# Two more gather slots in the latents' residual buffer for the first 56 gathers, and the residual loaded at step 30

## The chip, the cores and the metric

One Trainium2 chip, one of its cores. The metric is the device time of one execution in microseconds, median of the runs shown; lower is better. The engines are TensorE (PE in the profile), VectorE (DVE), ScalarE (ACT), GpSimd (POOL) and SyncE (SP, which here only issues transfers). The data is float32 throughout.

## The reference, cut to what matters

One inference layer over two sequences: 128 context tokens (the prompt) and 512 latent tokens (the sample), 640 tokens in all, in five blocks of 128. Each token goes through a token mixer (an SSM and a short gated convolution) and then through PEER, a retrieval of single-neuron experts:

```python
def layer(x, cond, h0_f, h0_b, rows, p):
    sh1, sc1, g1, sh2, sc2, g2 = [m.astype(x.dtype) for m in modulation(cond, p["w_mod"], p["b_mod"])]
    h = rmsnorm(x, p["norm1_g"]) * (1 + sc1) + sh1
    y, h_f, h_b = token_mixer(h, h0_f, h0_b, rows, p)
    x = x + g1 * y                                   # the residual that the change is about
    h = rmsnorm(x, p["norm2_g"]) * (1 + sc2) + sh2
    x = x + g2 * peer(h, p["w_query"], p["sub_keys"], p["expert_u"], p["expert_v"])
    return x, h_f, h_b

def block(xb):                                       # peer, one block of 128 tokens
    q = (xb @ w_query)...                            # 8 heads, two halves
    s = jnp.einsum("thse,sne->thsn", q, sk)
    ...                                              # top 16 of each half, then top 16 of the 256 sums
    gate = jax.nn.softmax(top, axis=-1)
    hid = jnp.einsum("thkd,td->thk", expert_u[idx], xb).astype(jnp.float32)
    act = (jax.nn.gelu(hid) * gate).astype(xb.dtype)
    return jnp.einsum("thk,thkd->td", act, expert_v[idx])
```

For every block, head and rank k one row of 2048 numbers (expert_u and expert_v of one expert, 8 KB) is fetched for each of 128 tokens. That is 5 x 8 x 16 = 640 gathers of 1 MB.

## The kernel before, in words

The program is written by hand, engine by engine; each engine runs its list in order and waits on semaphores. There are three stages.

The first (to about 213 us) computes the modulation, the SSM's matrices, the context's mixer and the context's residual. The second is the PEER of the context block (G = 0 to 7, one G for each head) with the latents' mixer laid between its pieces. The third is the PEER of the four latent blocks (G = 8 to 39).

**The gathers.** GpSimd issues the 640 gathers in order (L1890), each into one of SLOTS = 8 slots of 8 KB per partition in `r1`: gather j goes into slot j modulo 8. Before it is issued, GpSimd waits until `v_done` says that the slot's last row is used up. VectorE takes the first half of each row in a dot product with the token's hidden vector (`dot`, L1707), which waits for the row to land. Two rows make a pair. ScalarE applies GELU (L1258), VectorE weighs the pair (`weigh`, L1716 and L1719), and TensorE adds the second halves into two banks (`add_rows`, L846), which sets `v_done`. So a row's slot is free when TensorE has done its pair. In this text pair n holds gathers 2n and 2n + 1; a head has 8 pairs.

**The latents' mixer between them.** In the context block TensorE does, after the matmuls of pair n, step n of `latent_front`: a slice of the latents' projections (L930, L951), and from step 28 a slice of the output projection (L964). It also computes the next heads' queries there: `query(u)` (L781) needs the weights of head u, which are loaded into one buffer, `wqb`. VectorE has its own `latent_front(n)` after its dots; at n = 36 it forms for the first time residual + gate x output (L1788), in the buffer `xtl`, after a wait for `ld_xl`.

**SyncE's list.** All other loads are issued by SyncE in one fixed order with waits between them. The latents' residual `xtl` (2 MB, 128 x 8 runs of 512 numbers) is loaded when the context's output projection no longer needs its place (`zoc_mm` of 2): `xtl` shares the upper 4096 columns of `x_r` with half of the output weights, `woB`. Then follow the query weights of heads 1 and 2 (L443) and, for n = 0 to 63, the loads of `w_tiles` (L449), of query weights at n = 5, 13, 21, 29 (head n // 8 + 3) and of `w_o` (L453, n = 34 to 37). The query weights are 1 MB as 128 x 8 runs of 256 numbers. Each of these waits until its buffer is free; heads 2 to 8 wait for the previous query (`q_mm`).

Of the kernel before, what the change touches and what calls it, by code (L numbers as in the profile page):

```python
# [8 lines left out]
ALU = mybir.AluOpType  # L9
# [70 lines left out]
def build(nc, xT, condT, cols, w_mod, w_u, w_tiles, w_o, ssm, bc, dskip, skT, w_query, table, y_out, st_out, kfull):  # L80
    ctx = ExitStack()
    with ctx:
# [14 lines left out]
        def part(r, a, n):  # L97
            return r[:, a:a + n]
# [57 lines left out]

        rows = part(r1, 0, SLOTS * 2 * D).rearrange("p (s x) -> p s x", s=SLOTS)
        peer = part(r2, 0, 1024)
# [71 lines left out]
        ld_dsk = sem("ld_dsk")  # L230
        ld_sk = sem("ld_sk")
        ld_woa = sem("ld_woa")
        ld_wob = sem("ld_wob")
        ld_wob0 = sem("ld_wob0")
        ld_xc = sem("ld_xc")
        ld_xl = sem("ld_xl")
        ld_wq0 = sem("ld_wq0")
        ld_wq = sem("ld_wq")
# [115 lines left out]
        wtl_in = [sem(f"wtl_in{i}") for i in range(3)]  # L354
        row_in = [sem(f"row_in{i}") for i in range(SLOTS)]

# [17 lines left out]
        def _(sp):  # L374
# [24 lines left out]
            sp.dma_start(dsk[0:NCH, :], dskip).then_inc(ld_dsk, 16)  # L399
            sp.dma_start(sk[:, :, :], skT).then_inc(ld_sk, 16)  # L400
            for n in range(8, 18):
# [16 lines left out]
            sp.wait_ge(m_mm, 2)  # L418
            sp.dma_start(wqa, w_query[:, :, 0:DQ]).then_inc(ld_wq0, 16)
            for q in range(8, 10):  # L420
                load_conv_ctx(q)
            sp.wait_ge(mod_mm, 24)
            sp.dma_start(woA, w_o[:, 0:4, :, :]).then_inc(ld_woa, 16)
            for q in range(10, 12):
                load_conv_ctx(q)
            sp.wait_ge(zc_mm, 10)
            sp.dma_start(woB[:, 2:4, :, :], w_o[:, 6:8, :, :]).then_inc(ld_wob0, 16)
            sp.wait_ge(zc_mm, 12)
            sp.dma_start(woB[:, 0:2, :, :], w_o[:, 4:6, :, :]).then_inc(ld_wob, 16)
            sp.wait_ge(scan_ctx, 1)  # L430
            sp.dma_start(st_out, fin[:, :, :]).then_inc(st_dma, 16)
            sp.wait_ge(zoc_mm, 2)
            sp.dma_start(xtl, xT[:, :, CTX:T]).then_inc(ld_xl, 16)

# [47 lines left out]
        def _(pe):  # L482
# [276 lines left out]

            pe.wait_ge(ld_woa, 16)  # L760
            pe.wait_ge(ld_wob0, 16)
            out_ctx(True, range(KS), 1)
# [22 lines left out]
            def first_query():  # L785

                pe.wait_ge(ld_wq0, 16)
                for k in range(KD):
                    if k < KS:
                        pe.wait_ge(h_ready, KD + k + 1)  # L790
                    elif k == KS:
                        pe.wait_ge(xsc_ready, 2)
                    for h in range(2):
                        last = mm(bank[2][:, h * P:(h + 1) * P], wqa[:, k, h * P:(h + 1) * P], hT[:, k, 0:CTX], start=(k == 0 and h == 0),
                                  stop=(k == KD - 1), skip_group_check=True)
                last.then_inc(q_mm, 1)
# [39 lines left out]
            def add_rows(G, g):  # L836

                b = G // HEADS
                if G % HEADS == 0 and g == 0:
                    pe.wait_ge(h2c_ready, NH2 * (b + 1))  # L840
                pe.wait_ge(wgt_ready, NPR * G + g + 1)
                for h in range(2):
                    for e in range(2):
                        k = 2 * g + e
                        to = TG * ((k + 2 * h) % NTG)
                        last = mm(bank[ACC[b % 2][h]][to:to + TG, :], wgt[:, g % 2, e, :], rows[:, k % SLOTS, D + h * 512:D + (h + 1) * 512],  # L846
                                  start=(G % HEADS == 0 and k < NTG), stop=(G % HEADS == HEADS - 1 and k >= TOPK - NTG))
                        if h:
                            last.then_inc(v_done, 1)
# [177 lines left out]

            pe.wait_ge(ld_sk, 16)
            first_query()
# [51 lines left out]
        def _(act):  # L1081
# [200 lines left out]
            def take_sums(b):  # L1282

                act.wait_ge(v_done, (b + 1) * HEADS * TOPK + SLOTS)
# [116 lines left out]
        def _(dve):  # L1401
# [299 lines left out]
            def dot(G, par, k):  # L1701

                s, tg = k % SLOTS, k % NTG
                if G % HEADS == 0 and k < NTG:
                    dve.wait_ge(h2c_ready, G // HEADS * NH2 + tg + 2)
                dve.wait_ge(row_in[s], G * 32 + (k // SLOTS + 1) * 16)
                V.tensor_tensor_reduce(rows[:, s, 0:D], rows[:, s, 0:D], h2r[tg], 1.0, 0.0, ALU.mult, ALU.add,  # L1707
                                       hid[:, par, k:k + 1]).then_inc(dot_done, 1)

            def weigh(G, par, g):  # L1710

                n = NPR * G + g
                wl = Chain(dve, act_done, n)
                dve.wait_ge(gelu_done, n + 1)
                a = gel[:, par, 2 * g:2 * g + 2]
                wl(tt(a, a, gate[:, par, 2 * g:2 * g + 2], ALU.mult))  # L1716
                if n >= 2:
                    dve.wait_ge(v_done, 2 * (n - 1) + SLOTS)
                tt(wgt[:, g % 2, :, :], fold[:, :].rearrange("p (a m) -> p a m", a=1).broadcast_to([P, 2, TG]),  # L1719
                   a.rearrange("p (g m) -> p g m", m=1).broadcast_to([P, 2, TG]), ALU.mult).then_inc(wgt_ready, 1)  # L1720
# [111 lines left out]
            fl(V.tensor_copy(eyes[:, 1, 64:P], ident[:, 0:64]))  # L1832
            dve.wait_ge(v_done, NALL * TOPK + SLOTS)
            for h in range(2):
# [20 lines left out]
        def _(pool):  # L1855
# [12 lines left out]
            for a in range(2):  # L1868
                for b in range(2):
# [12 lines left out]
                           ident[:, :].rearrange("p (g s i) -> p g s i", g=NTG, s=1).broadcast_to([P, NTG, 4, TG])).then_inc(consts, 1)  # L1882
            pool.sem_inc(v_done, SLOTS)
            for G in range(NALL):
                e = G % 2
                pool.wait_ge(topk_done, G + 1)
                for k in range(TOPK):
                    pool.wait_ge(v_done, G * TOPK + (k + 1))
                    pool.nop(nofuse=True)
                    G_.indirect_dma_start(rows[:, k % SLOTS, :], None, table,  # L1890
                                          bass.IndirectOffsetOnAxis(gidx[:, e, k:k + 1], 0)).then_inc(row_in[k % SLOTS], 16)
    return nc
# [62 lines left out]
```

## Time and profile before

| | |
|---|---|
| median of 3 runs | 1960.12 us |
| lowest and highest | 1955.56 and 1962.29 us |
| span of the profiled execution | 1954.5 us |
| own time of the profiled execution | not given beside its span |
| PE, DVE, ACT, POOL busy | 61%, 73%, 19%, 37% |
| gathered | 671.13 of 745.91 MB |

The span runs from the first to the last instruction. The times are of whole executions, so the median is 5.6 us above this span; what lies between them holds the start and the end of the program and the difference between one execution and another. Part 2 of the page shows the span in 40 slices of 48.9 us; in it the transfer engines stand at 9 (90% or more) from slice 6 to the last but one. A share of 1.00 in a row of windows means that the 16 transfer engines were busy throughout.

### The profile page before, as it was taken

To read this page: it belongs to the slowest core of one execution; us is meant where nothing else is said; L and a number is where in the kernel's file an instruction comes from. 1 tells how busy PE (TensorE), PEld (TensorE's weight loads), DVE (VectorE), ACT (ScalarE), POOL (GpSimd) and SP (SyncE) were. 2 spreads that over 40 slices of the span, in tenths; PEclk is the share of its full clock that TensorE was granted. 3 is DMA by queue.
4 is the path that set the end of the run, shared out by engine and by line. 5 is a ranking of instruction groups with operands and counts; after the bars stand their busy time and mean duration, and the time that the engine had idled before them with its cause. 6 is when DMAs were issued, how large, how long until landed. Compare 5 with 4: busy or idle time off the path is not lost.

```text
span 1954.5 us, 22601 instructions
## 1 busy us (share of the span) xinstructions
PE 1197.1 (61%) x7716; PEld 476.1 (24%) x7716; DVE 1423.2 (73%) x3894; ACT 373.2 (19%) x845; POOL 717.9 (37%) x666
## 2 busy tenths in 40 slices
PE   6999888999767767774553434453444454444434
PEld 3569544444322322220110000111000011111001
DVE  8978557777766776667777777777777678877775
ACT  5242431221122111111211011121111111211010
POOL 0000233333333333334444444444444444344442
PEclk9999999999878777775755555565555565555555
DMA  8556799999999999999999999999999999999996
GB/s 347 179 196 220 275 358 401 373 396 415 401 368 374 404 414 401 397 401 393 421 421 422 419 410 416 412 412 412 416 413 415 417 412 415 415 410 419 412 409 254
DMA packets 126243, 745.91 MB, mean 382 GB/s; under 512 B 12128, under 2 KB 34912, under 8 KB 40624
## 3 DMA queue, kind: packets, MB, share of 16 engines
q0 software_dynamic: 92160, 671.13, 83.8%
q1 hardware_dynamic: 33968, 73.35, 10.5%
q8 instruction: 60, 0.98, 0.2%
q14 instruction: 55, 0.45, 0.1%
HBM read 741.78 MB, written 2.65 MB: 381 GB/s over the span
## 4 chain that ended last, share of the span: by engine, by line
DMA 33%; PE 30%; DVE 24%; issue 10%; ACT 1%; SPq 0%; DVEq 0%; POOL 0%; POOLq 0%; ACTq 0%
DMA r<-table,gidx 29%; DVE r L1707 8%; PE bank L846 7%; PE bank L814 6%; PE bank L951 3%; DMA r<-w_query 3%; PE bank L964 2%; PE bank L543 2%; DMA r<-w_u 2%; PE bank L781 1%; DVE wgt L1719 1%; DVE i L1649 1%; DVE r L1675 1%; DVE i L1655 1%; DVE r L1650 1%
## 5 line engine op out<-in xcount | busy, mean ns | idle before, releaser
L1890 POOL DMA_INDIRECT r<-table,gidx x640 | 709.7, 1109 | 1053.1 <-PE bank L846 891.0
L1707 DVE CUSTOM_DVE_ANT_0 r<-r 128x1024 f32<-128x1024 f32 x640 | 780.3, 1225 | 310.4 <-DMA r<-table,gidx 292.8
L846 PE MATMUL bank<-r,wgt 128*32 128x512 f32 x2560 | 532.2, 916 | 711.3 <-DVE wgt L1719 692.2
L846 PEld LDWEIGHTS bank<-r,wgt 128*32 128x32 f32 x2560 | 61.3, 130 | 1078.5 <-DVE wgt L1719 1011.3
L1258 ACT ACTIVATE r<-r 128x2 f32<-128x2 f32 x320 | 65.1, 204 | 1033.3 <-DVE r L1707 1016.4
L814 PE MATMUL bank<-hT_r,r 128*128 128x512 f32 x256 | 120.1, 624 | 0.9 <-ACT hT_r L1112 0.9
L1716 DVE TENSOR_TENSOR r<-r 128x2 f32<-128x2 f32 x320 | 50.1, 157 | 68.5 <-ACT r L1258 68.5
L1719 DVE TENSOR_TENSOR wgt<-fold,r 128x64 f32<-128x64 f32 x320 | 72.0, 225 | 11.1
L814 PEld LDWEIGHTS bank<-hT_r,r 128*128 128x128 f32 x256 | 50.0, 200 | 75.1 <-issue 75.1
L1258 ACT ACT_TABLE_LOAD x51 | 65.4, 1283 | 0.9
L964 PE MATMUL bank<-mix_r,r 128*128 128x512 f32 x128 | 61.0, 619 | 0.0
L951 PE MATMUL bank<-hT_r,r 128*128 128x512 f32 x128 | 60.8, 619 | 0.0
L832 PEld LDWEIGHTS bank<-r,ident 128*32 128x32 f32 x1280 | 43.0, 139 | 46.6 <-DVE r L1686 39.8
L1707 DVE DVE_READ_ACCUMULATOR2_ANT r<- 128x1 f32 x640 | 52.8, 83 | 0.0
L1254 ACT ACT_TABLE_LOAD x40 | 51.3, 1283 | 0.7
L871 PE MATMUL bank<-mix_r,modrow 128*128 128x512 f32 x80 | 47.4, 730 | 3.2 <-ACT r L1273 1.9
L832 PE MATMUL bank<-r,ident 128*32 128x8 f32 x1280 | 46.7, 195 | 1.5 <-DVE r L1686 1.5
L1648 DVE MAX8 r<-r 128x8 f32<-128x128 f32 x80 | 19.3, 284 | 23.8 <-ACT r L1250 15.9
L1875 POOL MEMSET r<- 128x2048 f32 x1 | 1.8, 1812 | 92.8 <-DVE sv L1506 92.8
L1254 ACT ACTIVATE r<-r,small 128x16 f32<-128x16 f32 x40 | 12.3, 308 | 114.8 <-DVE pos L1668 114.8
L543 PE MATMUL bank<-hT_r,r 128*128 128x512 f32 x64 | 32.5, 654 | 2.2 <-DMA r<-w_u 2.2
L781 PE MATMUL bank<-hT_r,r 128*128 128x128 f32 x224 | 29.3, 288 | 6.5 <-DMA r<-w_query 6.5
(356 smaller groups left out, 1438.5 us busy)
## 6 DMA issues: line engine op xcount, KB each, us to landing
r<-w_mod SPq DMA_DIRECT2D x24, 1024.0 KB, 8.2
r<-w_query SPq DMA_DIRECT2D x15, 1024.0 KB
r<-table,gidx POOLq DMA_INDIRECT x640, 11.7
r<-w_tiles SPq DMA_DIRECT2D x12, 512.0 KB, 8.2
x_r<-w_tiles SPq DMA_DIRECT2D x10, 512.0 KB, 5.9
hT_r<-xT SPq DMA_DIRECT2D x4, 640.0 KB, 5.9
r<-w_u SPq DMA_DIRECT2D x1, 2048.0 KB, 29.9
r<-w_o SPq DMA_DIRECT2D x1, 2048.0 KB, 10.9
```

Source lines behind the costliest of these rows:

```text
L543: last = mm(bank[m][:, :], wu[:, k, m * P:(m + 1) * P], hT[:, k, CTX:T], start=(k == 0), stop=(k == KD - 1))
L814: last = mm(bank[2 + h][:, :], wqb[:, k, h * P:(h + 1) * P], hT[:, k, CTX:T], start=(k == 0), stop=(k == KD - 1))
L832: last = mm(bank[3][TG * s:TG * s + TG, 8 * tg:8 * tg + 8], ident[:, TG * tg:TG * tg + TG], gi[:, :, 4 * s:4 * s + 4], start=True, stop=True)
L846: last = mm(bank[ACC[b % 2][h]][to:to + TG, :], wgt[:, g % 2, e, :], rows[:, k % SLOTS, D + h * 512:D + (h + 1) * 512], start=(G % HEADS = ...
L951: last = mm(bank[(4, 5, 7)[r]][:, :], wtl[(tile + 2) % 3][:, k, :], hT[:, k, CTX:T], start=(k == 0), stop=(k == KD - 1))
L964: last = mm(bank[OUT_BANK[m % 3]][:, :], woA[:, m % 4, k, :], mixl[:, k, :], start=(k == 0), stop=(k == KD - 1))
L1254: A(e16, top, ACT.Exp, bias=small[:, 0:1], accum_out=small[:, 1:2]).then_inc(exp_done, 1)
L1258: A(gel[:, par, 2 * g:2 * g + 2], hid[:, par, 2 * g:2 * g + 2], ACT.Gelu_apprx_tanh).then_inc(gelu_done, 1)
L1707: V.tensor_tensor_reduce(rows[:, s, 0:D], rows[:, s, 0:D], h2r[tg], 1.0, 0.0, ALU.mult, ALU.add, hid[:, par, k:k + 1]).then_inc(dot_done, 1)
L1716: wl(tt(a, a, gate[:, par, 2 * g:2 * g + 2], ALU.mult))
L1719: tt(wgt[:, g % 2, :, :], fold[:, :].rearrange("p (a m) -> p a m", a=1).broadcast_to([P, 2, TG]), a.rearrange("p (g m) -> p g m", m=1).bro ...
L1890: G_.indirect_dma_start(rows[:, k % SLOTS, :], None, table, bass.IndirectOffsetOnAxis(gidx[:, e, k:k + 1], 0)).then_inc(row_in[k % SLOTS], 16)
```

## The change

Two more slots are made out of the place of `xtl`. A table that is made when the program is built (`slot_ring`) gives each gather its slot, the slot's use count and the gather that had it before. Gathers 0 to 55 go round 10 slots, the rest round 8. For the first 56 gathers the slot of gather j was last held by gather j - 10. Gathers 56 and 57 take over slots from 46 and 47, gather 58 from 50, and from there the previous holder is always j - 8, as before. The last gather in one of the two extra slots is 49.

The load of `xtl` goes from its place after `zoc_mm` to SyncE's step n = 30, behind the query weights of n = 29, with a wait for `v_done` of 50. The first gather into each extra slot waits for `zoc_mm` of 2 instead. Some semaphores are merged (`ld_sk` with `ld_wq0`, `ld_woa` with `ld_wob0`) and the starting credit of 8 on `v_done` goes away, with every wait on it lowered by 8.

```diff
+EARLY = 2
+EARLY_TO = 56
+def slot_ring(total):
+    last, slot, use, prev = {}, [], [], []
+    for j in range(total):
+        s = min(range(SLOTS + EARLY if j < EARLY_TO else SLOTS), key=lambda i: last.get(i, i - SLOTS - EARLY))
+        slot.append(s)
+        use.append(slot.count(s))
+        prev.append(last.get(s))
+        last[s] = j
+    return slot, use, prev
...
-        rows = part(r1, 0, SLOTS * 2 * D).rearrange("p (s x) -> p s x", s=SLOTS)
+        rows = [part(r1, 2 * D * i, 2 * D) for i in range(SLOTS)] + [part(x_r, D, 2 * D), part(x_r, 3 * D, 2 * D)]
+        SLOT, USE, PREV = slot_ring(NBLK * HEADS * TOPK)
...
-            sp.wait_ge(zoc_mm, 2)
-            sp.dma_start(xtl, xT[:, :, CTX:T]).then_inc(ld_xl, 16)
...
+                if n == 30:
+                    sp.wait_ge(v_done, max(j for j in range(EARLY_TO) if SLOT[j] >= SLOTS) + 1)
+                    sp.dma_start(xtl, xT[:, :, CTX:T]).then_inc(ld_xl, 16)
...
-            pe.wait_ge(ld_woa, 16)
-            pe.wait_ge(ld_wob0, 16)
+            pe.wait_ge(ld_wo, 32)
...
-                dve.wait_ge(row_in[s], G * 32 + (k // SLOTS + 1) * 16)
-                V.tensor_tensor_reduce(rows[:, s, 0:D], rows[:, s, 0:D], h2r[tg], 1.0, 0.0, ALU.mult, ALU.add,
+                dve.wait_ge(row_in[SLOT[j]], USE[j] * 16)
+                V.tensor_tensor_reduce(row, row, h2r[tg], 1.0, 0.0, ALU.mult, ALU.add,
...
-            pool.sem_inc(v_done, SLOTS)
...
-                    pool.wait_ge(v_done, G * TOPK + (k + 1))
+                    j = G * TOPK + k
+                    if PREV[j] is not None:
+                        pool.wait_ge(v_done, PREV[j] + 1)
+                    elif SLOT[j] >= SLOTS:
+                        pool.wait_ge(zoc_mm, 2)
```

SyncE's list before, from the loads of the context's output weights to the last `w_tiles`. The residual is `x_r<-xT 128x8x512`, the query weights are `w_query`:

```order
L429 DMA x_r<-w_o 128x2048 [waits zc_mm]
L431 DMA st_out<-fin 128x64 [waits scan_ctx]
L433 DMA x_r<-xT 128x8x512 [waits zoc_mm]
L443 DMA r<-w_query 128x8x256 [waits yl_mm]
L443 DMA r<-w_query 128x8x256 [waits q_mm]
L449 DMA mix_r<-w_tiles 128x1024
```

And the same list after the change, with the end of this stretch:

```order
L442 DMA x_r<-w_o 128x2048 [waits zc_mm]
L444 DMA st_out<-fin 128x64 [waits scan_ctx]
L454 DMA r<-w_query 128x8x256 [waits yl_mm]
...
L460 DMA r<-w_tiles 128x1024 [waits zl_mm] x2
L454 DMA r<-w_query 128x8x256 [waits q_mm] x2
L475 DMA x_r<-xT 128x8x512 [waits v_done]
L464 DMA r<-w_o 128x1024 [waits zol_mm] x4
L454 DMA r<-w_query 128x8x256 [waits q_mm] x2
```

The residual has moved past two loads of query weights in front of it, twelve of `w_tiles` and four more of query weights, to just behind the query weights of n = 29 and ahead of the four pieces of `w_o`.

GpSimd's list before, from the first gather:

```order
L1890 DMA r<-table,gidx 128x2048 [waits topk_done,v_done]
L1890 DMA r<-table,gidx 128x2048 [waits v_done] x15
L1890 DMA r<-table,gidx 128x2048 [waits topk_done,v_done]
L1890 DMA r<-table,gidx 128x2048 [waits v_done] x15
```

And after; a gather into `x_r` is one into an extra slot:

```order
L1906 DMA r<-table,gidx 128x2048 [waits topk_done]
L1906 DMA r<-table,gidx 128x2048 x7
L1906 DMA x_r<-table,gidx 128x2048 [waits zoc_mm] x2
L1906 DMA r<-table,gidx 128x2048 [waits v_done] x6
L1906 DMA r<-table,gidx 128x2048 [waits topk_done,v_done]
L1906 DMA r<-table,gidx 128x2048 [waits v_done]
L1906 DMA x_r<-table,gidx 128x2048 [waits v_done] x2
```

Gathers 8 and 9 no longer wait for the first pair's matmuls but only for `zoc_mm`; the order of the gathers is the same.

## Rows read from the trace of the kernel before

**Rows 1.** The page, parts 2 and 4: slices of the span, and the last chain.

```profile
DMA  8556799999999999999999999999999999999996
GB/s 347 179 196 220 275 358 401 373 396 415 401 368 374 404 414 401 397 401 393 421 421 422 419 410 416 412 412 412 416 413 415 417 412 415 415 410 419 412 409 254
DMA 33%; PE 30%; DVE 24%; issue 10%; ACT 1%; SPq 0%; DVEq 0%; POOL 0%; POOLq 0%; ACTq 0%
```

**Rows 2.** Windows: stretch, busy us of each engine, clock, transfer share, GB/s.

```profile
200.00:213.00 13.00, 12.18 (x280) 10.21 (x281) 8.67 (x37) 5.91 (x10) 0.00 (x0) 1.00 0.02 4
255.00:280.00 25.00, 23.98 (x143) 12.97 (x143) 11.26 (x33) 5.39 (x11) 8.66 (x8) 0.97 0.83 305
280.00:320.00 40.00, 38.17 (x205) 18.20 (x205) 31.14 (x79) 8.68 (x17) 13.89 (x13) 1.00 1.02 415
320.00:380.00 60.00, 53.58 (x254) 23.93 (x251) 40.76 (x107) 10.96 (x22) 19.31 (x18) 0.94 0.97 368
416.00:424.00 8.00, 8.00 (x31) 2.87 (x24) 3.55 (x8) 0.77 (x3) 4.22 (x4) 1.00 0.99 351
424.00:450.00 26.00, 23.92 (x137) 9.97 (x136) 23.59 (x73) 7.29 (x14) 12.15 (x11) 1.00 1.01 421
450.00:505.00 55.00, 53.49 (x274) 27.10 (x273) 37.62 (x98) 9.09 (x22) 19.07 (x18) 0.97 1.02 415
700.00:1925.00 1225.00, 587.59 (x3229) 149.42 (x3227) 903.61 (x2526) 176.06 (x429) 530.57 (x477) 0.57 1.01 412
```

**Rows 3.** The last chain in order of time: start, us, what; pieces of it.

```profile
225.68 26.98 DMA r<-w_query
252.70 3.78 PE bank L781 x16
...
377.23 30.00 DMA r<-w_query
407.27 2.05 PE bank L781 x16
...
715.25 9.72 DMA r<-table,gidx
```

**Rows 4.** Waits of DVE, 225 to 452 us: us, times, longest.

```profile
DVE r L1707 <- DMA r<-table,gidx: 1.6, 2, 1.3
```

**Rows 5.** Waits of DVE, 700 to 1925 us.

```profile
DVE r L1707 <- DMA r<-table,gidx: 248.0, 233, 2.2
```

**Rows 6.** Waits of PE, 225 to 452 us.

```profile
PE bank L781 <- DMA r<-w_query: 6.5, 2, 5.0
```

**Rows 7.** Timeline of SP: start, us, what (x2: first to last issue).

```profile
190.23 0.55 SPq L433 DMA_DIRECT2D x_r<-xT  x1
...
377.23 39.08 SPq L443 DMA_DIRECT2D r<-w_query  x2
```

**Rows 8.** Transfer queues, 226 to 252 us: packets, MB, share.

```profile
q0 software_dynamic: 1193, 8.66, 80.3%
q1 hardware_dynamic: 1309, 2.03, 21.6%
```

**Rows 9.** Transfer queues, 416 to 424 us.

```profile
q1 hardware_dynamic: 1031, 1.04, 41.7%
```

**Rows 10.** Timeline of PE around 407 us; in brackets idle before, and releaser.

```profile
402.09 3.70 PE L951 MATMUL bank<-hT_r,r 128*128 128x512 f32 x8
407.27 2.05 PE L781 MATMUL bank<-hT_r,r 128*128 128x128 f32 x16 [1.48 <-DMA r<-w_query]
```

**Rows 11.** Timeline of DVE, 448 to 465 us.

```profile
448.92 1.40 DVE L1788 SCALAR_TENSOR_TENSOR x_r<-bank,modT,x_r 128x512 f32<-128x512 f32 x2
...
452.15 1.22 DVE L1707 CUSTOM_DVE_ANT_0 r<-r 128x1024 f32<-128x1024 f32 x1 [0.70 <-DMA r<-table,gidx]
...
457.60 1.23 DVE L1707 CUSTOM_DVE_ANT_0 r<-r 128x1024 f32<-128x1024 f32 x1 [3.21 <-DMA r<-table,gidx]
...
461.20 1.23 DVE L1707 CUSTOM_DVE_ANT_0 r<-r 128x1024 f32<-128x1024 f32 x1 [2.37 <-DMA r<-table,gidx]
...
462.54 0.22 DVE L1719 TENSOR_TENSOR wgt<-fold,r 128x64 f32<-128x64 f32 x1
```

**Rows 12.** Timeline of PE, 459 to 464 us.

```profile
459.15 3.70 PE L964 MATMUL bank<-mix_r,r 128*128 128x512 f32 x8
462.82 1.06 PE L846 MATMUL bank<-r,wgt 128*32 128x512 f32 x8
```

**Rows 13.** Timeline of POOL, the eighth, ninth and fifteenth gather.

```profile
222.57 0.94 POOL L1890 DMA_INDIRECT r<-table,gidx  x1 [0.30 <-issue]
232.85 1.20 POOL L1890 DMA_INDIRECT r<-table,gidx  x1 [9.34 <-PE bank L846]
...
258.34 0.94 POOL L1890 DMA_INDIRECT r<-table,gidx  x1 [10.34 <-PE bank L846]
```

**Rows 14.** The page, part 6: median us from issue to landing.

```profile
r<-table,gidx POOLq DMA_INDIRECT x640, 11.7
```

More of the change, by code:

```diff
@@ L230, in build @@
         ld_dsk = sem("ld_dsk")
-        ld_sk = sem("ld_sk")
-        ld_woa = sem("ld_woa")
+        ld_wo = sem("ld_wo")
         ld_wob = sem("ld_wob")
-        ld_wob0 = sem("ld_wob0")
         ld_xc = sem("ld_xc")
         ld_xl = sem("ld_xl")
-        ld_wq0 = sem("ld_wq0")
+        ld_first = sem("ld_first")
         ld_wq = sem("ld_wq")
@@ L354, in build @@
         wtl_in = [sem(f"wtl_in{i}") for i in range(3)]
-        row_in = [sem(f"row_in{i}") for i in range(SLOTS)]
+        row_in = [sem(f"row_in{i}") for i in range(SLOTS + EARLY)]
         NPR = TOPK // 2
@@ L399, in _ @@
             sp.dma_start(dsk[0:NCH, :], dskip).then_inc(ld_dsk, 16)
-            sp.dma_start(sk[:, :, :], skT).then_inc(ld_sk, 16)
+            sp.dma_start(sk[:, :, :], skT).then_inc(ld_first, 16)
             for n in range(8, 18):
@@ L418, in _ @@
             sp.wait_ge(m_mm, 2)
-            sp.dma_start(wqa, w_query[:, :, 0:DQ]).then_inc(ld_wq0, 16)
+            sp.dma_start(wqa, w_query[:, :, 0:DQ]).then_inc(ld_first, 16)
             for q in range(8, 10):
@@ L422, in _ @@
             sp.wait_ge(mod_mm, 24)
-            sp.dma_start(woA, w_o[:, 0:4, :, :]).then_inc(ld_woa, 16)
+            sp.dma_start(woA, w_o[:, 0:4, :, :]).then_inc(ld_wo, 16)
             for q in range(10, 12):
@@ L426, in _ @@
             sp.wait_ge(zc_mm, 10)
-            sp.dma_start(woB[:, 2:4, :, :], w_o[:, 6:8, :, :]).then_inc(ld_wob0, 16)
+            sp.dma_start(woB[:, 2:4, :, :], w_o[:, 6:8, :, :]).then_inc(ld_wo, 16)
             sp.wait_ge(zc_mm, 12)
@@ L785, in first_query @@
             def first_query():
-                pe.wait_ge(ld_wq0, 16)
+                pe.wait_ge(ld_first, 32)
                 for k in range(KD):
@@ L845, in add_rows @@
                         to = TG * ((k + 2 * h) % NTG)
-                        last = mm(bank[ACC[b % 2][h]][to:to + TG, :], wgt[:, g % 2, e, :], rows[:, k % SLOTS, D + h * 512:D + (h + 1) * 512],
+                        last = mm(bank[ACC[b % 2][h]][to:to + TG, :], wgt[:, g % 2, e, :], rows[SLOT[G * TOPK + k]][:, D + h * 512:D + (h + 1) * 512],
                                   start=(G % HEADS == 0 and k < NTG), stop=(G % HEADS == HEADS - 1 and k >= TOPK - NTG))
@@ L1026, in turn_last @@
                         last.then_inc(pt_mm, 1)
-            pe.wait_ge(ld_sk, 16)
             first_query()
@@ L1282, in take_sums @@
             def take_sums(b):
-                act.wait_ge(v_done, (b + 1) * HEADS * TOPK + SLOTS)
+                act.wait_ge(v_done, (b + 1) * HEADS * TOPK)
                 if b:
@@ L1701, in dot @@
             def dot(G, par, k):
-                s, tg = k % SLOTS, k % NTG
+                j, tg = G * TOPK + k, k % NTG
+                row = rows[SLOT[j]][:, 0:D]
                 if G % HEADS == 0 and k < NTG:
                     dve.wait_ge(h2c_ready, G // HEADS * NH2 + tg + 2)
-                dve.wait_ge(row_in[s], G * 32 + (k // SLOTS + 1) * 16)
-                V.tensor_tensor_reduce(rows[:, s, 0:D], rows[:, s, 0:D], h2r[tg], 1.0, 0.0, ALU.mult, ALU.add,
+                dve.wait_ge(row_in[SLOT[j]], USE[j] * 16)
+                V.tensor_tensor_reduce(row, row, h2r[tg], 1.0, 0.0, ALU.mult, ALU.add,
                                        hid[:, par, k:k + 1]).then_inc(dot_done, 1)
@@ L1717, in weigh @@
                 if n >= 2:
-                    dve.wait_ge(v_done, 2 * (n - 1) + SLOTS)
+                    dve.wait_ge(v_done, 2 * (n - 1))
                 tt(wgt[:, g % 2, :, :], fold[:, :].rearrange("p (a m) -> p a m", a=1).broadcast_to([P, 2, TG]),
@@ L1832, in _ @@
             fl(V.tensor_copy(eyes[:, 1, 64:P], ident[:, 0:64]))
-            dve.wait_ge(v_done, NALL * TOPK + SLOTS)
+            dve.wait_ge(v_done, NALL * TOPK)
             for h in range(2):
@@ L1887, in _ @@
                 for k in range(TOPK):
-                    pool.wait_ge(v_done, G * TOPK + (k + 1))
+                    j = G * TOPK + k
[3 more added lines that the diff above has]
+                        pool.wait_ge(zoc_mm, 2)
                     pool.nop(nofuse=True)
-                    G_.indirect_dma_start(rows[:, k % SLOTS, :], None, table,
-                                          bass.IndirectOffsetOnAxis(gidx[:, e, k:k + 1], 0)).then_inc(row_in[k % SLOTS], 16)
+                    G_.indirect_dma_start(rows[SLOT[j]], None, table,
+                                          bass.IndirectOffsetOnAxis(gidx[:, e, k:k + 1], 0)).then_inc(row_in[SLOT[j]], 16)
     return nc
```

## The prediction

> **What bounds the kernel now.** I read the page first. The transfer engines are at 90% or more from the sixth slice on and move 400 to 420 GB/s in most slices after the fifteenth [rows 1], so a change that moves transfers looks as if it touched the bound. But the last chain gives DMA only 33% of the span, PE 30% and DVE 24% [rows 1], so the bound must change on the way. I therefore took the chain in order of time. From 213 to about 700 us its pieces are almost all PE and DVE; the only transfers in it are two loads of query weights, at 225.68 and 377.23 us [rows 3]. The first gathered row in it stands at 715.25 us [rows 3], and from there on rows alternate with short compute to the end. The waits say the same. Between 225 and 452 us VectorE, which takes the rows, waited for one only twice, 1.6 us in all [rows 4]. Between 700 and 1925 us it waited 233 times, 248.0 us [rows 5].
>
> So there are two regimes. In the last 1225 us the transfers bind: share 1.01, 412 GB/s [rows 2]. In the context's heads (213 to some 550 us) TensorE's list binds: it is busy 38.17 of 40 us and 53.49 of 55 us in two of the windows [rows 2], with the latents' mixer laid between the pairs. The transfer engines are nearly full there too, but have holes: 305 GB/s in 255 to 280, 368 in 320 to 380, 351 in 416 to 424 [rows 2]. The change acts in that second regime only. What it does to the end is what it does to the moment at which the compute chain hands over to the transfers, near 700 us.
>
> **The change part by part.**
>
> *Two more slots.* Before, GpSimd issued the eighth gather at 222.57 us and then waited 9.34 us for the first pair's matmuls; the fifteenth waited 10.34 us and was issued at 258.34 [rows 13]. Now gathers 8 and 9 follow at once and every pair until 28 is issued one pair earlier. That fills holes: at 415 GB/s as in the full window 280 to 320 [rows 2], those of 255 to 280 and 320 to 380 are worth 25 x (1 - 305/415) = 6.6 us and 60 x (1 - 368/415) = 6.8 us. But the lead can never be more than the two rows, 2.1 MB or 5.05 us, and nobody waits for it: VectorE's waits for rows here sum to 1.6 us [rows 4], and neither stands on the chain. Bounds 0 and -1.6 us; I take 0. The lead also ends by itself. Gather 58 waits for the matmuls of gather 50, as it did before, so the lead is spent by about 395 us.
>
> *The query weights behind the gathers.* TensorE waits twice for them, 6.5 us in all, 5.0 us of it before 252.70 [rows 3, 6]. Does a longer queue of gathers make this worse? In 226 to 252 us the gathers' queue had 1193 packets and SyncE's 1309, though 8.66 MB against 2.03 MB [rows 8]: while both have work they take turns piece by piece, 8 KB against 1 KB. A load of 1024 pieces waits its 1024 turns however many gathers stand behind, so two more don't lengthen it, and the 5.0 us stay. Bounds: 0 to +5 us (two rows, if the load had to wait for both); I take 0, by the counts. The second wait is 1.48 us before 407.27 [rows 10]. Its load was on its way from 377.23 for 30.00 us [rows 3]. Now the gathers' queue runs dry under it for a few us, since rows up to 57 were moved early and gather 58 is held as before; without gathers in between, the load gets through faster. Bounds 0 and -1.5 us; I take -1.5.
>
> *The residual's load.* Before it was issued at 190.23 us [rows 7] into idle engines (200 to 213 us: share 0.02, [rows 2]) and cost nothing. Now it is issued behind the second of the two query loads of the row at 377.23, that is at 377.23 + 39.08 = 416.3 us [rows 7]. Its wait for `v_done` of 50 is over by then, since pair 24 is long done, so nothing behind it on SyncE's queue (the `w_o` pieces) waits longer to be issued. It is 2.10 MB, at 421 GB/s of the window behind [rows 2] 5.0 us of transfer time in a stretch that was full: 421 and 415 GB/s until 505 us [rows 2]. What was idle there after 416 us: 8 x (1 - 351/421) = 1.3 us. So 5.0 - 1.3 = 3.7 us of it push rows back. Who waits for those rows? From 452 us on VectorE does: 0.70, 3.21 and 2.37 us [rows 11]. And there TensorE has no slack: the pair that VectorE weighed at 462.54 was taken at 462.82, the moment the matmuls before it ended [rows 11, 12]. So I count the 3.7 us in full. Bounds: 0 (the slack of VectorE over TensorE takes it up) and +5.0 us.
>
> *The residual itself.* VectorE needs it at 448.92 us [rows 11]. The query weights in front of it were through at 424: 1.04 of their 1.05 MB moved in 416 to 424 [rows 9], in the hole. From there 1024 pieces take turns with the gathers, as did the 1 MB load that took 26.98 us [rows 3]; 2 KB pieces instead of 1 KB add 1.05 MB or 2.5 us. 27.0 + 2.5 = 29.5 us from issue, of which about 2 us lie before the first byte, so it lands near 424 + 27.5 = 451.5 us, some 3 us late (4 if the chain came there 1.5 us early). VectorE then stands, with its dots behind, but these had waited 0.70 + 3.21 us for their rows anyway [rows 11]. Bounds 0 and +15 us (rival C); I take +0.5.
>
> The rule that bears on this is in the Trainium skill, DMA: Bandwidth & Descriptors, section on queues, rings and completion order: each transfer engine goes round the queues that have work and changes at packet boundaries. The counts of [rows 8] agree with it. By the rule the load lands near 451 us; by a share in bytes it would land far later, which is rival C.
>
> *Merged semaphores and the lower counts:* no instruction more on an engine, and the merged loads were long there. 0 us. GpSimd's wait for `zoc_mm` of 2 is over before its first gather, since the same wait had let the old load go at 190.23 [rows 7].
>
> Sum: 0 - 1.5 + 3.7 + 0.5 = +2.7 us, made against the span of 1954.5 us: 1957.2. In the last regime every row waits for the one before it, so a shift at 700 us reaches the end whole. The median of the runs is 5.6 us above the span (1960.12), so I forecast 1962.8, rounded 1963 us.
>
> **The rivals.**
>
> *A, the forecast:* 1963 us.
>
> *B, the transfers bind already in the context's heads.* For it: share 0.97 to 1.02 nearly throughout [rows 2], and GpSimd waits for slots. Then the two rows of lead count in full, -5.05 us, with -1.5 us for the query weights, and the moved load costs what the holes leave, between 0 and 3.7 us. That is -6.6 to -2.9: about 1955 us. Against it: the row waits of 1.6 us, and a lead that is spent by gather 58.
>
> *C, the residual comes late.* If the queues share by bytes and not by turns, 2 MB take 2 x 27 = 54 us from 424 and VectorE stops at 448.92. Then the slots fill and no gather follows. What is left are some 4 to 5 rows under way (11.7 us from issue to landing, [rows 14]) and 1.1 MB of the residual, 2.7 us: it lands near 464, a stop of 15 us, of which the row waits of 6.3 us [rows 11] hide part. After it the transfers stand until a pair has gone through. It decides from the point where landing passes 455 us, where the row waits no longer cover it. Some +12 us: 1972. Against it: the packet counts [rows 8].
>
> *D, the late rows are taken up* by the distance VectorE keeps ahead of TensorE. Only the query weights count, -1.5: 1958.6, no change to be seen.
>
> **How the numbers follow.** A 0.53, D 0.20, C 0.14, B 0.13. The likeliest is A, so 1963. A measurement of this kernel can tell about 0.3%, 5.9 us, from no change: faster is below 1954.2, slower above 1966.0. B's lower half lies below, and runs spread by 6.7 us: faster 0.10. C lies above, and the end of A where its terms take their upper bounds (5.0 + 3): slower 0.21. Same 0.69. The range leaves out C's end and B's best: 1955 to 1971; A's own range is 1958 to 1968.
>
> **What would show it.** In the new profile: gathers 8 and 9 issued near 224 and 225 us; the windows 255 to 280 and 320 to 380 nearer to 415 GB/s, with TensorE at the same places of its list at the same times; query at 252.70 unchanged, and the wait at 407.27 gone; the residual issued near 415 us and L1788 first at 450 to 453; more waiting for rows between 440 and 470; the first row of the chain near 717 us instead of 715.25. I am wrong if the pair behind step 20 is earlier by several us (B), if L1788 starts after 455 us (C), or if the late rows don't show at pair 37 (D).

## The result, and the profile after

| | before | after |
|---|---|---|
| median, 18 runs each | 1959.25 us | 1966.36 us |
| lowest and highest | 1950.79, 1963.28 us | 1959.51, 1969.65 us |
| span of the profiled execution | 1954.5 us | 1964.4 us |
| ratio of the runs | | 1.0038, 95% interval 1.0027 to 1.0049 |

The change makes the kernel slower by 0.38%, 7.4 us (5.3 to 9.6). The forecast was +2.7 us and 1963 us, in a range of 1955 to 1971. The sign held, and so did the place and the cause of the loss as far as the experiments below show them; the size was too small.

The lines of the kernel after stand 13 further down in these parts: L781, L846, L951, L1707 and L1788 of before are L794, L859, L964, L1720 and L1801 of after.

The page of the kernel after, parts 2 and 4, against [rows 1]:

```profile
DMA  9455799999999999999999999999999999999996
GB/s 357 167 202 187 280 375 401 372 359 415 406 351 381 394 416 395 399 394 380 421 420 422 415 413 416 415 411 413 415 416 414 414 411 413 417 413 411 420 411 258
DMA 35%; PE 31%; DVE 21%; issue 10%; ACT 1%; SPq 0%; DVEq 0%; POOL 0%; POOLq 0%; ACTq 0%
```

The fourth slice (147 to 195 us) has fallen from 220 to 187 GB/s, since the residual has left it, and slices 5 and 6 have risen from 275 and 358 to 280 and 375. The slices from 20 on look alike: both kernels are at the transfers' limit there.

GpSimd's timeline after, around the first extra slots, against [rows 13]:

```profile
221.09 0.94 POOL L1906 DMA_INDIRECT r<-table,gidx  x1 [0.30 <-issue]
222.33 1.14 POOL L1906 DMA_INDIRECT x_r<-table,gidx  x1 [0.30 <-issue]
223.78 0.94 POOL L1906 DMA_INDIRECT x_r<-table,gidx  x1 [0.31 <-issue]
234.03 0.93 POOL L1906 DMA_INDIRECT r<-table,gidx  x1 [9.31 <-PE bank L859]
```

Gathers 8 and 9 go out at once; the wait of 9 us has only moved to gather 10. The windows after, against [rows 2] (stretch, busy us of each engine, clock, transfer share, GB/s):

```profile
255.00:280.00 25.00, 23.98 (x139) 12.25 (x139) 10.96 (x32) 5.38 (x11) 8.39 (x8) 0.94 0.88 337
320.00:380.00 60.00, 53.84 (x262) 24.31 (x261) 39.88 (x104) 11.23 (x23) 19.71 (x18) 0.94 0.97 374
380.00:410.00 30.00, 28.13 (x160) 12.67 (x160) 27.43 (x78) 8.14 (x15) 8.40 (x8) 1.00 0.95 364
416.00:424.00 8.00, 8.00 (x30) 2.84 (x23) 3.73 (x8) 0.94 (x3) 4.05 (x4) 1.00 0.93 314
424.00:450.00 26.00, 20.84 (x125) 8.72 (x127) 19.76 (x63) 7.09 (x13) 11.11 (x9) 1.00 1.02 416
```

The early holes are filled a little (305 to 337 and 368 to 374 GB/s). What was moved ahead is missing later: a new hole in 380 to 410 us. And in 424 to 450 us TensorE, busy 23.92 us before, has only 20.84 us of work.

SyncE's timeline after, and VectorE's between 441 and 467 us:

```profile
379.17 37.31 SPq L454 DMA_DIRECT2D r<-w_query  x2
416.52 0.67 SPq L475 DMA_DIRECT2D x_r<-xT  x1
```

```profile
441.81 1.23 DVE L1720 CUSTOM_DVE_ANT_0 r<-r 128x1024 f32<-128x1024 f32 x1 [0.61 <-DMA r<-table,gidx]
...
448.02 1.23 DVE L1720 CUSTOM_DVE_ANT_0 r<-r 128x1024 f32<-128x1024 f32 x1 [1.72 <-DMA r<-table,gidx]
...
454.46 1.40 DVE L1801 SCALAR_TENSOR_TENSOR x_r<-bank,modT,x_r 128x512 f32<-128x512 f32 x2
...
459.08 1.22 DVE L1720 CUSTOM_DVE_ANT_0 r<-r 128x1024 f32<-128x1024 f32 x1 [2.08 <-DMA r<-table,gidx]
```

The residual goes out at 416.5 us. Behind 420 us the first row that is waited for is now at 441.81 instead of 452.15 us. The residual landed 31.5 us after its issue, at 448.0 us; when VectorE comes to L1801 at 454.46 it is there, and no wait is marked. The transfer queues of the kernel after (packets, MB, share), first 416 to 424 us, then 424 to 452 us:

```profile
q1 hardware_dynamic: 1124, 1.26, 53.7%
q0 software_dynamic: 184, 1.25, 38.8%
...
q0 software_dynamic: 1333, 9.75, 83.9%
q1 hardware_dynamic: 956, 1.89, 17.8%
```

SyncE's queue (q1) moved 3.15 MB in these 36 us, the query weights of head 6 and the residual.

**The chain, pair by pair.** The best ruler in these traces is the start of the last matmul of each pair (L846 before, L859 after), which is at the same place in TensorE's list in all kernels. I took it from each trace; the table gives the difference to before in us. Of the experiments below, those with ten slots stand first.

| kernel | pair 4 | pair 10 | pair 26 | pair 28 | pair 36 | pair 41 | from 26 to 41 | row waits 424 to 480 us |
|---|---|---|---|---|---|---|---|---|
| before | 0 | 0 | 0 | 0 | 0 | 0 | 0 | 9.8 |
| after | +0.3 | +2.0 | +1.9 | +0.2 | +3.4 | +5.4 | +3.5 | 14.3 |
| after, again (6) | -0.7 | -0.7 | -0.7 | -2.5 | +1.5 | +3.9 | +4.6 | 15.8 |
| slots only (2) | +0.1 | +0.1 | +0.1 | -1.6 | -1.6 | -0.4 | -0.5 | 5.4 |
| slots, step 28 (3) | -0.7 | +0.9 | +0.8 | -0.9 | -0.9 | -2.4 | -3.2 | 8.6 |
| slots, half load (4) | -2.3 | -2.3 | -2.4 | -4.1 | -2.8 | +1.4 | +3.8 | 13.7 |
| slots, step 34 (8) | +0.2 | +0.2 | +0.2 | -1.6 | +20.2 | +18.6 | +18.4 | 0 |
| move only (1) | -3.5 | -1.8 | -1.9 | -1.9 | +3.0 | +1.5 | +3.4 | 13.7 |
| 8 slots, step 28 (7) | -2.3 | -0.6 | -0.7 | -0.4 | +0.1 | +2.7 | +3.4 | 11.5 |
| two query buffers (5) | -2.5 | -0.8 | -0.9 | -2.6 | -2.6 | -3.1 | -2.2 | 9.6 |
| two query buffers (9) | -4.8 | -4.8 | -4.7 | -6.5 | -6.0 | -3.8 | +0.9 | 10.9 |

The numbers in brackets are those of the experiments. The last column is VectorE's waiting for gathered rows. Behind pair 41 single profiles drift apart by more than the effect: between pairs 41 and 128 the kernel after lost 6.0 us more than the profile of before, but so did the same kernel with the load left out (11.2 us), and its median is not above before. The one profile of before was a quick one in that stretch. The profiled executions of experiments 2, 3 and 7 were the slowest of their twelve. So the medians are the measure of the whole and the chain up to pair 41 shows the place.

### The profile page after: what moved, and what is told of

It reads as the page before. It is cut to its first block, busy times and chain, and to the rows that moved or that the text cites. A ratio compares the mean times of both kernels' runs of the same rounds, so it can differ in the third digit from the quotient of the medians.

```text
span 1964.4 us, 22593 instructions
## 1 busy us (share of the span) xinstructions
PE 1199.7 (61%) x7716; PEld 475.1 (24%) x7716; DVE 1421.6 (72%) x3894; ACT 373.3 (19%) x845; POOL 726.4 (37%) x666
## 4 chain that ended last, share of the span: by engine, by line
DMA 35%; PE 31%; DVE 21%; issue 10%; ACT 1%; SPq 0%; DVEq 0%; POOL 0%; POOLq 0%; ACTq 0%
DMA r<-table,gidx 32%; DVE r L1720 7%; PE bank L859 7%; PE bank L827 6%; PE bank L964 4%; PE bank L977 2%; PE bank L557 2%; DMA r<-w_u 2%; DMA r<-w_query 1%; DVE wgt L1732 1%; PE bank L794 1%; DVE i L1661 1%; PE bank L884 1%; PE bank L656 1%; DVE i L1667 1%
## 5 line engine op out<-in xcount | busy, mean ns | idle before, releaser
L1720 DVE CUSTOM_DVE_ANT_0 r<-r 128x1024 f32<-128x1024 f32 x630 | 768.0, 1224 | 316.4 <-DMA r<-table,gidx 300.5
L859 PE MATMUL bank<-r,wgt 128*32 128x512 f32 x2520 | 527.7, 923 | 716.3 <-DVE wgt L1732 715.9
L859 PEld LDWEIGHTS bank<-r,wgt 128*32 128x32 f32 x2520 | 60.4, 130 | 1079.8 <-DVE wgt L1732 1033.2
L964 PE MATMUL bank<-hT_r,r 128*128 128x512 f32 x128 | 61.5, 624 | 0.0
L1720 DVE DVE_READ_ACCUMULATOR2_ANT r<- 128x1 f32 x640 | 52.3, 82 | 0.0
L1255 ACT ACTIVATE r<-bank 128x512 f32<-128x512 f32 x16 | 9.6, 597 | 120.5 <-PE bank L827 120.5
```

The costliest lines, as they stand in the source:

```text
L964: last = mm(bank[(4, 5, 7)[r]][:, :], wtl[(tile + 2) % 3][:, k, :], hT[:, k, CTX:T], start=(k == 0), stop=(k == KD - 1))
L1720: V.tensor_tensor_reduce(row, row, h2r[tg], 1.0, 0.0, ALU.mult, ALU.add, hid[:, par, k:k + 1]).then_inc(dot_done, 1)
```

## The experiments

Each ratio is to runs of the kernel before on the same chip, taken with it. R1 to R5 are the rival explanations named in the expectations.

**1. The move alone.** The changed kernel with 8 slots throughout.

```diff
-EARLY = 2
+EARLY = 0
...
-                    sp.wait_ge(v_done, max(j for j in range(EARLY_TO) if SLOT[j] >= SLOTS) + 1)
+                    sp.wait_ge(zoc_mm, 2)
```

> The residual's load at step 30 as in the changed kernel, but with the 8 slots of before for all gathers. My theory (the 2 MB pushed into a full stretch cost, the slots bring nothing but the 1.5 us of the query weights at 407 us): +5.5 to +7 us against before, ratio 1.003 to 1.0035; the wait of TensorE at 407 us is there again. Rival R1 (the two more slots cost, by more gathers in front of every other load): 0 to +2 us. Rival R2 (both together): +3 us.

Measured: 1962.52 us against 1957.93, ratio 1.0016 (0.9998 to 1.0034), +3.1 us (-0.4 to +6.7). In the chain +3.4 us between pairs 26 and 41, all of it behind pair 31, and the row waits of 424 to 480 us rise from 9.8 to 13.7 us. So the move by itself makes the late rows that the kernel after has. TensorE's wait for query weights is there again (1.43 us before 405.34). The cost is less than the 5.5 to 7 I expected. The interval takes in no change and both rivals (0 to +2 and +3 us), so the median alone doesn't show a cost; the chain does.

**2. The slots alone.** The load is left out, so the latents' residual is not added, and VectorE waits for `v_done` of 50 in place of `ld_xl`.

```diff
-                if n == 30:
-                    sp.wait_ge(v_done, max(j for j in range(EARLY_TO) if SLOT[j] >= SLOTS) + 1)
-                    sp.dma_start(xtl, xT[:, :, CTX:T]).then_inc(ld_xl, 16)
...
-                        dve.wait_ge(ld_xl, 16)
+                        dve.wait_ge(v_done, 50)
```

> The two more slots for 56 gathers, and the residual's load left out (the sum at L1788 of the first kernel takes what stands in the buffer, so the latents' output is not the reference's). My theory: -3 to 0 us against before, likeliest -1.5, since TensorE no longer waits for query weights at 407 us and the early rows bring nothing. R1: +5 to +7 us. A theory by which early rows are worth their 5 us: -5 or more.

Measured: 1957.32 us, ratio 0.9995 (0.9977 to 1.0013), -1.0 us (-4.5 to +2.5). The chain is -1.6 us at pair 28, where TensorE no longer waits for query weights, and level everywhere before (+0.1): 26 pairs whose rows are fetched up to two gathers ahead move nothing. At pair 41 only -0.4 is left. R1, by which the slots cost the 5 to 7 us, is refuted.

**3. The load two steps earlier.**

```diff
-                if n == 30:
+                if n == 28:
```

> The changed kernel with the residual's load at step 28, ahead of the query weights of head 6, so that it goes out near 392 us, when gather 49 is used up. In the changed kernel the engines moved 364 GB/s in 380 to 410 us and 336 and 314 in the two windows behind, a hole of 6.7 us at 415 GB/s; the load is 5.0 us. My theory: the hole takes it, -1.5 to +1.5 us against before. Rival R3 (the bytes cost wherever they stand in the gathers' time): +7 us, as the changed kernel.

Measured: 1958.53 us, ratio 0.9998 (0.9983 to 1.0012), -0.4 us (-3.3 to +2.4). The load now goes out ahead of the query weights of head 6. SyncE's timeline of this kernel:

```profile
391.33 0.54 SPq L475 DMA_DIRECT2D x_r<-xT  x1
414.85 0.54 SPq L454 DMA_DIRECT2D r<-w_query  x1
```

Windows of 380 to 424 us, of the kernel after and of this one:

```profile
380.00:424.00 44.00, 42.13 (x214) 19.05 (x215) 33.94 (x92) 9.14 (x18) 14.32 (x14) 1.00 0.94 351
```

```profile
380.00:424.00 44.00, 42.01 (x214) 19.31 (x210) 32.96 (x90) 9.44 (x20) 14.82 (x14) 1.00 1.02 405
```

The same bytes went into the hole (351 to 405 GB/s; 54 GB/s x 44 us = 2.4 MB), the row waits fell back to 8.6 us, and the 7.4 us are gone. R3 is refuted: the bytes do not cost wherever they stand. That the hole is the reason is argued from the windows; experiment 7 tests it and doesn't settle it.

**4. Half the load.** The other half of the buffer keeps old rows.

```diff
-                    sp.dma_start(xtl, xT[:, :, CTX:T]).then_inc(ld_xl, 16)
+                    sp.dma_start(xtl[:, 0:4, :], xT[:, 0:4, CTX:T]).then_inc(ld_xl, 16)
```

> The changed kernel with only half of the residual loaded (4 of 8 slices, 1 MB; the other half of the buffer keeps old rows, so the output is not the reference's). My theory (transfer time of the bytes): half of the load's cost, +2.5 to +4.5 us against before. Rival R4 (a fixed cost of the wait or of a load behind the query weights): +6 to +7.5 us. Rival R5 (the load lands too late for its first user and only that costs): 0 to +1 us, since half the pieces land some 13 us earlier.

Measured: 1962.03 us, ratio 1.0023 (1.0006 to 1.0039), +4.5 us (+1.2 to +7.6). By the median half the load costs something between nothing much and all of it; the chain gives +3.8 us from pair 26 to 41, no less than the full load, and 13.7 us of row waits against 14.3. A cost that goes with the bytes is not shown by this run, and R4, a fixed cost, is not refuted by it: its +6 to +7.5 us overlap the interval. R5, by which only a late residual costs, is refuted by the interval and by the trace of the kernel after, where L1801 waited for no load.

**5. Another use of the place.** 8 slots; the query weights of heads 2 and 4 are loaded into the residual's place, those of heads 3 and 5 one head earlier, the residual at step 22.

```diff
-EARLY = 2
+EARLY = 0
+XL_AT = 22
...
+        wqx = part(x_r, D, 2048).rearrange("p (k m) -> p k m", k=KD)
...
+                if u in (2, 4):
+                    sp.wait_ge(*((zoc_mm, 2) if u == 2 else (q_mm, 3)))
+                    sp.dma_start(wqx, w_query[:, :, u * DQ:(u + 1) * DQ]).then_inc(ld_wx, 16)
+                    return
...
+            load_query(2)
             load_query(1)
-            load_query(2)
+            load_query(3)
...
-                if n == 30:
-                    sp.wait_ge(v_done, max(j for j in range(EARLY_TO) if SLOT[j] >= SLOTS) + 1)
+                if n == XL_AT:
+                    sp.wait_ge(q_mm, 5)
...
-                if n % NPR == 5:
+                if n in (5, 13):
+                    load_query(n // NPR + 4)
+                if n % NPR == 5 and n > 21:
```

> The residual's place used for something that stands on the chain: the query weights of heads 2 and 4 go into it (head 2 at once, at 190 us, into idle engines), the weights of heads 3 and 5 are then loaded one head earlier, and the residual is loaded at step 22, when head 4's query is done (near 372 us); 8 slots throughout. TensorE's two waits for query weights (5.0 us before 252.70 and 1.5 us before 407.27 in the first kernel) should both go. My theory: the chain is shorter by 5 to 6.5 us at pair 28, the residual's load costs 0 to 3.5 us of it: -6.5 to -2 us against before, likeliest -4 (ratio 0.998). Rival (transfers bind in this stretch, so a chain that runs 5 us ahead waits for rows instead): -1 to +3 us.

Measured: 1956.51 us against 1960.48, ratio 0.9979 (0.9965 to 0.9993), -4.1 us (-6.9 to -1.4). The first kernel that is faster than before, and the rival (-1 to +3 us) is refuted. Its chain is only -2.5 us at pair 4; see experiment 9.

**6. The changed kernel again.** No edit.

> The changed kernel once more, with a second profile, beside the others of this call. At pair 28 its chain lay +0.2 us against before, at pair 41 +5.4, of which 3.5 us came between pairs 26 and 41 and 2.0 us between pairs 8 and 10, where TensorE's clock fell for some us. My theory: the 3.5 us between pairs 26 and 41 come again (within 0.7), the 2.0 us come or don't, as they did in other kernels' profiles; +5 to +9 us against before in the median. Rival (the two slots cause the slower stretch at pair 9): 2.0 us there again.

Measured: 1967.66 us, ratio 1.0037 (1.0018 to 1.0055), as the first time. Between pairs 26 and 41 the chain lost 4.6 us (3.5 the first time, 1.1 apart and so outside the 0.7 I allowed). The step at pair 9 (+0.3 to +2.0 us, so 1.7, in the first profile) did not come again, and experiments 1, 5 and 7 have a step of 1.7 there with 8 slots: the slots do not cause it.

**7. Step 28 with 8 slots.**

```diff
-                if n == 30:
+                if n == 28:
```

in the kernel of experiment 1.

> The residual's load at step 28 with 8 slots throughout, where it follows the query weights of head 5 at 378 us at once. With 8 slots the engines were full in 380 to 410 us (414 GB/s in the first kernel) and the hole of 380 to 424 that the ten slots leave is not there, only the one of 410 to 424 (2.6 us). My theory (a load costs its bytes less the holes): +2 to +4 us of chain between pairs 26 and 41 and in the median; with ten slots (experiment 3) it was -3.2 us of chain there and -0.4 us in the median. Rival (only the distance to the first user counts, and any load well before step 36 is free): -1 to +1 us.

Measured: 1958.11 us, ratio 0.9997 (0.9980 to 1.0014), -0.6 us (-3.9 to +2.7). The load followed the query weights of head 5 at 377.24 us. The chain gave what I expected, +3.4 us between pairs 26 and 41, most of it at pair 37 (+0.1 before, +2.7 after), but the median doesn't confirm it: it lies within the rival's -1 to +1 us, by which any load well before step 36 is free. So a load into full engines shows in the chain and not for certain in the whole; that the hole left by the ten slots is what makes step 28 free there is not settled.

**8. The residual too late.** The load behind the first piece of `w_o`.

```diff
-                if n == 30:
+                if n in (34, 35, 36, 37):
+                    load_out_lat(n - 30)
+                if n == 34:
                     sp.wait_ge(v_done, max(j for j in range(EARLY_TO) if SLOT[j] >= SLOTS) + 1)
                     sp.dma_start(xtl, xT[:, :, CTX:T]).then_inc(ld_xl, 16)
-                if n in (34, 35, 36, 37):
-                    load_out_lat(n - 30)
```

> The changed kernel with the residual's load behind the first piece of w_o at step 34, which goes out when VectorE is about to need the residual (near 450 us). This makes rival C of the prediction come true, to see its price and how the queues share when a user stands. My theory: from some 452 us VectorE stands at L1801, the gathers under way (4 to 5 rows, 10 to 12 us) and the 2 MB (5 us) then go through side by side, it starts near 468 us; as the row waits of some 6 us are under it, the chain at pair 41 is +12 to +18 us against before and the median +11 to +17. Rival (the load keeps taking turns with gathers for all its 1024 pieces): landing 27 us after issue, L1801 near 480 us, +22 us or more.

Measured: 1982.48 us against 1961.76, ratio 1.0109 (1.0081 to 1.0137), +21.4 us (+15.9 to +26.9). VectorE's timeline of this kernel:

```profile
469.80 1.41 DVE L1801 SCALAR_TENSOR_TENSOR x_r<-bank,modT,x_r 128x512 f32<-128x512 f32 x2 [22.36 <-DMA x_r<-xT]
```

Its windows of 460 to 470 and 470 to 480 us:

```profile
460.00:470.00 10.00, 0.00 (x0) 0.00 (x0) 0.20 (x1) 0.00 (x0) 0.00 (x0) 0.50 1.02 401
470.00:480.00 10.00, 9.40 (x34) 4.84 (x35) 7.13 (x15) 1.72 (x5) 0.00 (x0) 0.73 0.07 25
```

Issued at 447.17, landed at 469.8: 22.6 us, a few us less than the 27 of the rival, as the gathers stopped. The chain was -1.6 us at pair 35 and +20.2 at pair 36. I had 12 to 18 at pair 41. The time of landing was right within 2 us. What I had taken off for the row waits came off only in part: VectorE waited for no row at all between 440 and 520 us (13.3 us before), yet the chain got back only 1.6 us, from +20.2 to +18.6; most of those waits had not been on it. In 470 to 480 us the transfer engines moved 25 GB/s, because all slots were full of rows not yet used; the chain to pair 41 shows no price for that.

**9. The kernel of experiment 5 again.** No edit to it.

> The kernel of experiment 5 (query weights of heads 2 and 4 in the residual's place, residual at step 22, 8 slots) once more, with a second profile. The first gave 0.9979 [0.9965, 0.9993] against before and a chain of -2.6 us at pair 28, less than the -5 to -6.5 expected, since TensorE's clock was at half for some us from 214 to 240, in which it lost 3.6 to 4.8 us that it had not lost in the first kernel. My theory: -2.5 to -7 us in the median; where the clock holds in this stretch, pair 4 lies at -4 us or earlier. Rival (the gain at pair 4 is bounded by the rows and not by the weights): -2.5 us at pair 4 whatever the clock.

Measured: 1954.97 us against 1961.76, ratio 0.9968 (0.9952 to 0.9984), -6.3 us (-9.4 to -3.1). Here TensorE's clock was low for a shorter time around 235 us, and the chain stood at -4.8 us at pair 4 and -6.5 at pair 28, where the first profile had -2.5 and -2.6. The rival (a gain bounded by the rows at -2.5) is refuted. Between pairs 34 and 41 it gave 2.2 us back to late rows.

## Why the prediction was right, and where it was too small

*What bounds the kernel in the context's heads.* Right: the compute chain. Experiment 2 shows it. Its rows came earlier and its chain did not move by more than 0.1 us in 26 pairs. Rival B (transfers bind already) is refuted for gathers 8 to 57; from some 440 us on rows are waited for too, and there it holds in part.

*The query weights.* Right in both terms against the one profile of before. The load before 252.70 took 27.24 us after (26.98 before, [rows 3]). But that two more rows don't lengthen it is not so in general: with 8 slots, in experiments 1 and 7, the same load took 18.9 and 17.2 us, with ten slots 26.6 to 27.4 in all six profiles (last section). The medians of experiments 2 and 3 show no price of it. The wait at 407 us went, as its load took 22.4 us instead of 30.00. TensorE's timeline after, against [rows 10]:

```profile
404.01 3.70 PE L964 MATMUL bank<-hT_r,r 128*128 128x512 f32 x8
407.55 1.95 PE L794 MATMUL bank<-hT_r,r 128*128 128x128 f32 x16
```

No idle time is marked before 407.55, and the chain falls from +1.9 to +0.2 us: 1.7, where I had 1.5. All five other profiles with ten slots show it; experiments 1 and 7, with 8 slots, have the wait (1.43 and 1.77 us).

*The rows pushed back.* The step that was mis-sized. I counted 5.0 - 1.3 = 3.7 us for the residual's bytes and set the 1.5 us of the query weights against it. From pair 28 to 41 it was 5.2 us (and 6.4 the second time). Against experiment 2, the same kernel without the load (1.2 us in this stretch), the load itself cost 4.0 and 5.2 us, so 3.7 was near; what fails is to set the 1.5 us against it in full. The likeliest reason is that the two terms don't add: where rows are waited for, it is their landing that sets the pace, and a chain that comes there early waits the more. With 8 slots, and without the gain, the same stretch cost 3.4 us. In both forms the net between pairs 26 and 41 is about the same, 3.5 and 3.4 us (4.6 in the second profile of the changed kernel). So the net of -1.5 + 3.7 came out near +3.7. Experiment 2 shows the same without any load: of its -1.6 us 1.2 were gone at pair 41. But that an early chain loses its lead there is not a rule: experiment 9 came to pair 28 6.5 us early and still had 3.8 at pair 41, and experiment 5 kept all of its 2.6. The hole was also counted wrongly: I filled the 1.3 us that were idle before after 416 us, but the slots' lead had by then emptied the queue, and the new hole of 380 to 416 us lay ahead of the load, where it was of no use. Experiment 3 put the load into it, and the cost went; whether by the hole or by the two steps alone is open (experiment 7).

*The residual itself.* I had 0.5 us for a landing 3 us late, at 451.5. It landed at 448.0 us, 22.8 us after the query weights in front of it (425.2) and not 27.5, and so before the 448.92 at which it was needed in the kernel before; late rows then held VectorE back to 454.46. Rival C didn't come; experiment 8 gives its price, 21 us and not 12.

*The rest.* By the ratio the whole moved by 7.4 us, the chain at pair 41 by 5.4 and 3.9 in two profiles. In the first profile 1.7 us of it arose at pair 9, where the clock was low in this profile and not in the second (last section). The other 2 to 3 us lie behind pair 41 or in the spread of the runs; what makes them stays open. Nor does the cost go clearly with the bytes (experiment 4), and the median of experiment 7 doesn't follow its chain.

*A version that beats both* is that of experiments 5 and 9: the free place was of use to the loads that TensorE waits for, and not to the gathers. It was -4.1 and -6.3 us against before, which is 11 us and more against the changed kernel's +7.4. The gain in the median is shown twice. Where it comes from is shown at pair 28, where the wait of 1.5 us is gone; at pair 4 experiments 1 and 7 stand at -3.5 and -2.3 us without the second buffer, as the load landed early there too, so its share of the -2.5 and -4.8 us is not known.

## What to carry to other kernels

A deeper prefetch pays only where somebody waits for what it fetches; read the waits of the consumer in that stretch first, not the share of the transfer engines. A load that is free where it stands can cost its transfer time once it is moved into a full stretch where rows are waited for, and a lead in the chain ahead of that stretch need not pay for it. When a deeper buffer ends, it leaves a hole: try first to issue what has to be loaded late into that hole (here two steps earlier took the cost away).

## What the runs showed of the hardware

A wait of TensorE can cost more than its length. Before, TensorE waited 4.98 us for the query weights and then took 3.78 us for 16 matmuls, in the kernel of experiment 1, where it came there without waiting, 1.95 us. The two timelines, before and then experiment 1, and behind them the windows of 250 to 255 us with the granted clock (third from the end, 0.50 is 1.2 GHz and 1.00 is 2.4 GHz):

```profile
252.70 3.78 PE L781 MATMUL bank<-hT_r,r 128*128 128x128 f32 x16 [4.98 <-DMA r<-w_query]
```

```profile
251.14 1.95 PE L794 MATMUL bank<-hT_r,r 128*128 128x128 f32 x16
```

Before, the windows say:

```profile
250.00:255.00 5.00, 2.30 (x11) 2.30 (x11) 0.42 (x2) 2.74 (x3) 0.00 (x0) 0.50 1.01 418
```

And in experiment 1:

```profile
250.00:255.00 5.00, 5.00 (x31) 2.85 (x30) 3.97 (x9) 4.54 (x7) 1.71 (x2) 1.00 1.01 395
```

The low level stood after the wait, the high one where TensorE came without waiting; the same 16 matmuls differ by 1.8 us. The low level doesn't always follow: in the kernel after, behind a wait of 3.90 us, they took 2.48 us, with 0.97 in 250 to 255 us.

Experiment 1 had no wait there because its load landed 18.9 us after its issue, and not 27. The two transfer queues in 236 to 244 us, before and then experiment 1:

```profile
q0 software_dynamic: 371, 2.69, 80.9%
q1 hardware_dynamic: 517, 0.53, 19.1%
```

```profile
q0 software_dynamic: 282, 2.03, 62.1%
q1 hardware_dynamic: 835, 1.14, 40.7%
```

GpSimd issued the ninth gather of experiment 1 at 233.87 us, 1 us later than before ([rows 13]):

```profile
233.87 0.93 POOL L1906 DMA_INDIRECT r<-table,gidx  x1 [11.53 <-PE bank L859]
```

The gathers' queue moved less for a while (282 packets against 371), and the load got through (835 packets against 517). The gather was late because the matmuls of the first pair were: TensorE's granted clock was 0.51 in 230 to 240 us, against 1.00 before. In experiments 4 and 8 it was as low there (0.51 and 0.50), but they have ten slots, and the load took 26.6 and 27.4 us; at pair 4 they stand at -2.3 and +0.2 us, experiment 1 at -3.5. So two more gathers in the queue can cost TensorE's weights an early landing. How often a run goes one way or the other is not shown, nor what brought the low stretch on.

The same wait can be answered in two ways from run to run. At pair 8 TensorE waits 1.83 us in every profile, until VectorE has weighed the pair. In 295 to 300 us behind it, before, after, and after again:

```profile
295.00:300.00 5.00, 5.00 (x39) 2.74 (x36) 4.83 (x12) 0.21 (x1) 2.00 (x2) 1.00 1.02 418
```

```profile
295.00:300.00 5.00, 5.00 (x21) 3.05 (x14) 4.83 (x11) 0.20 (x1) 2.00 (x2) 0.66 1.03 414
```

```profile
295.00:300.00 5.00, 5.00 (x52) 2.52 (x51) 4.86 (x12) 0.20 (x1) 2.00 (x2) 1.00 1.02 408
```

Of these three only the first profile of the changed kernel has a low stretch (0.66), and its chain is 1.7 us later for it at pair 10. Experiments 1, 3, 5 and 7 lose the same 1.6 to 1.7 us there, with 8 slots as with ten. A difference of that size at one place needs a second profile.

The queues. Beside gathers throughout, 1 MB in 1024 pieces took 26.98, 27.24 and 30.00 us, and 2 MB in 1024 pieces 31.5 us (the residual after; 30.1 to 33.2 in experiments 1, 3, 5, 6 and 9). 1 MB in 512 pieces took 19.8 us (experiment 4). When the gathers stopped under way, the 2 MB took 22.6 us (experiment 8). In these runs a load's time beside a full queue goes more with its number of pieces than with its bytes.
